# Recurrence, mLSTM and block attention as pieces between the chunks of one stream of projections

## The reference

```python
xn = rms_norm_2(x, mix_norm_g)
parts = split(xn @ w_in_2)           # LRU x, z | mLSTM u, o, z, two gates | block attention q, k, v, z
lru  = rg_lru_branch(...)            # causal conv, two block-diagonal gates, scan over the tokens, * silu(z)
ml   = mlstm_branch(...)             # conv, silu, block-diagonal q, k, v; 4 heads of 192, chunks of 128
                                     # tokens; * sigmoid(o), layer norm of each head, * silu(z)
moba = attention(q, k, v, alibi) * silu(z)    # 6 heads of 128, one block of 256 tokens
x = x + concat(lru, ml, moba) @ w_out_2
```

## Time and profile before

| | us |
|---|---|
| median of 3 runs (2581.98 to 2593.54) | 2593.01 |
| the profiled execution's own time | 2587.25 |
| its span in the profile | 2585.4 |
| PE busy in the span | 2109.4 (82%) |
| DVE, ACT, POOL busy | 1323.9, 631.1, 617.5 |
| mean granted clock of PE | 0.94 |
| DMA moved | 723 MB, 280 GB/s over the span |

### The profile page before, as it was taken

One profiled execution on the slowest core, in us unless ns is written; L12 is line 12 of the kernel. 1 busy time (PEld: TensorE's weight loads), 2 busy tenths in 40 slices (PEclk: granted clock), 3 DMA queues, 4 the chain that ended last, 5 costly groups with the idle time before them and its releaser, 6 DMA issues. The chain is left out here.

```text
span 2585.4 us, 22666 instructions
## 1 busy us (share of the span) xinstructions
PE 2109.4 (82%) x8289; PEld 1394.9 (54%) x8289; DVE 1323.9 (51%) x1822; ACT 631.1 (24%) x927; POOL 617.5 (24%) x518
## 2 busy tenths in 40 slices
PE   5999868974898899677778889977888999845976
PEld 4878656862444444222234444432348999834874
DVE  3456437457455546455665545654323344366544
ACT  4434235221101111111111110110023333343333
POOL 0000000016454354344454354444310000000000
PEclk8999969996999999899999999999989999967988
DMA  4555501479999999999999999999954455600432
GB/s 169 193 191 191 178 1 52 144 280 377 422 419 420 422 420 422 422 422 421 421 420 414 422 417 418 421 421 422 392 170 170 148 183 182 196 6 25 166 128 81
DMA packets 101560, 723.39 MB, mean 280 GB/s; under 512 B 11712, under 2 KB 12864, under 8 KB 20704
## 3 DMA queue, kind: packets, MB, share of 16 engines
q0 software_dynamic: 73728, 536.90, 50.4%
q1 hardware_dynamic: 27744, 185.32, 20.5%
HBM read 720.08 MB, written 2.10 MB: 279 GB/s over the span
## 5 line engine op out<-in xcount | busy, mean ns | idle before, releaser
L1164 PE MATMUL bank<-ring,work 128*128 128x512 f32 x2048 | 951.7, 610 | 237.0 <-DMA ring<-in_peer_up_dram,work 233.3
L1370 DVE CUSTOM_DVE_ANT_0 ring<-ring,mix_t 128x2048 f32<-128x2048 f32 x256 | 584.3, 2292 | 527.6 <-DMA ring<-in_peer_down_dram,work 527.5
L1164 PEld LDWEIGHTS bank<-ring,work 128*128 128x128 f32 x2048 | 376.3, 193 | 744.8 <-issue 542.7
L400 DVE TENSOR_TENSOR ring_r<-ring,ring_r 128x2048 fp32r<-128x2048 f32 (+2 forms) x160 | 321.7, 2013 | 386.1 <-ACT ring_r L378 385.9
L443 PE MATMUL bank<-ring_r,mix_r 128*128 128x512 f32 (+1 forms) x1440 | 449.4, 377 | 12.1 <-ACT h L341 12.1
L1267 POOL DMA_INDIRECT ring<-in_peer_down_dram,work x256 | 325.6, 1272 | 451.0 <-DVE work L1337 243.8
L1276 POOL DMA_INDIRECT ring<-in_peer_up_dram,work x256 | 289.8, 1132 | 523.3 <-PE bank L1164 459.7
L443 PE MATMUL bank<-ring_r,act_r 128*128 128x512 f32 (+1 forms) x1152 | 395.9, 384 | 18.9 <-DVE ring_r L400 18.9
L378 ACT ACTIVATE ring_r<-ring 128x2048 fp32r<-128x2048 f32 (+2 forms) x160 | 270.1, 1690 | 445.0 <-DMA ring<-in_w_out_dram 90.4
L443 PEld LDWEIGHTS bank<-ring_r,mix_r 128*128 128x128 f32 x1440 | 269.3, 189 | 54.8 <-ACT h L341 13.0
L1222 ACT ACTIVATE work<-const,work 128x128 f32<-128x128 f32 x256 | 97.7, 399 | 772.5 <-PE bank L1164 770.4
(11 more groups left out here) (326 smaller groups left out, 1112.0 us busy)
## 6 DMA issues: line engine op xcount, KB each, us to landing
ring<-in_w_out_dram SPq DMA_DIRECT2D x32, 1024.0 KB, 4.8
ring<-in_w_in_qk_dram SPq DMA_DIRECT2D x24, 1024.0 KB, 4.9
ring<-in_w_in_rest_dram SPq DMA_DIRECT2D x24, 1024.0 KB, 4.9
ring<-in_w_in_mo_dram SPq DMA_DIRECT2D x24, 768.0 KB, 4.3
ring<-in_w_in_tok_dram SPq DMA_DIRECT2D x24, 768.0 KB, 4.3
h<-in_w_query_dram SPq DMA_DIRECT2D x8, 2048.0 KB, 11.7
h<-in_xa_wkv_dram SPq DMA_DIRECT2D x4, 2048.0 KB, 16.8
ring<-in_w_in_lru_dram SPq DMA_DIRECT2D x8, 1024.0 KB, 4.8
```

The source lines that it names most:

```text
L400: dve.tensor_tensor(low(s, job), raw, plain(high(s, job)), ALU.subtract).then_inc(k.weights_low, 1)
L1164: m = pe.matmul(B[c][:, :], diag[:, j % DEPTH, :], up_row(j)[:, c * 512:(c + 1) * 512], start=first, stop=last)
L1370: dve.tensor_tensor_reduce(down_row(j), down_row(j), xn[:, t, :], 1.0, 0.0, ALU.mult, ALU.add, dots[:, p, j:j + 1]).then_inc(down_used, 1)
```

## The change

**One stream.** `Stream` lays out chunks in order, each with its slot, its banks and, for each bank, the count at which it is free; PE waits for a bank only where it opens it. All loops are unrolled; this form serves every projection of the program. "in2" and "out2" become one call of `project` with 80 chunks: gates 0 to 3, LRU 4 to 11, mLSTM u 12 to 19 (now three groups of 128 features, 36 matmuls), mLSTM o and z 20 to 31 (three tok blocks of 512), attention v 32 to 39, attention q, k, z for three heads and again for the other three 40 to 63, output 64 to 79 with two blocks by turns. It has banks 0 to 3; the last two output blocks take 4 to 7, which the pieces use until then. Banks are evacuated three chunks after a block's last one in program order (before: four).

**Pieces.** Each stage's engine programs become generators that yield the tick of their next piece. `runner` does what is due ahead of a chunk: PE at tick t ahead of chunk t, ACT and DVE at tick t ahead of the split of chunk t+3, SP ahead of the load of chunk t+3. The order on each engine is thus fixed.

**Ticks.** Recurrence: DVE 1, 3, 8 and 9 (convolution in halves), 15, 17, 18; PE 12; ACT 2, 13 (sigmoids), 14 (tanh, exp), 15 (silu), 16 (square root). mLSTM: PE 5, 10, 15, 17, 20, 22, 26 to 37, 47; DVE 2, 4, 6, 9, 11, 16, 19 to 24 (convolution in halves at 22 and 24), 28, 30 to 36, 38 to 40, 42, 44 to 46, 48; ACT 7, 20 to 22, 24, 26, 27, 29, 36, 37, 41, 43, 48. Recurrence's result is split at 49. Attention: scores at 51, 52, 53, 60, 61, 62, on DVE and ACT at the same ticks, division one later, transposes two, second product three later, gates at 55, 55, 56, 64 to 66, splits at 57 and 67.

**Memory.** The pieces work in `h`, `work` and in `x` itself, so SP stores the 2 MB of `x` to DRAM at tick 0 (with six small loads) and loads it back at tick 47, behind the 1.5 MB of alibi and a wait for the mLSTM result. The mixed activations are split where they lie, per piece. Where a query head's 192 rows end inside a chunk of 128, the product uses a half filled with zeros (`k_half`, cleared by POOL).

**Elsewhere.** The loads of the memory's query weights start with the normalisation ahead of it (before: at the end of "out2").

```diff
-def load_chunks(sp, k, job, b, n, groups_done):
...
+class Stream:
...
+    def __init__(self, k, order, banks=range(8), late_banks=None):
...
+        for job, b, s in order:
+            c = Chunk(job, b, s)
+            c.n, c.slot = k.chunks, k.chunks % CHUNKS
+            c.load_wait = k.slot_free[c.slot]
...
+    def runner(self, eng, programs):
+        tasks = [[0, program(eng)] for program in programs]
+
+        def at(tick):
+            for task in tasks:
+                while task[0] <= tick:
+                    task[0] = next(task[1], math.inf)
...
         def _(sp):
...
+            at, rest = beside.runner(sp, beside.load)
+            for p in range(len(chunks)):
+                at(p - AHEAD)
+                if p >= stream.started:
+                    stream.load(sp, p)
...
         def _(act):
...
+            for p in range(len(chunks) + AHEAD):
+                at(p - AHEAD)
...
+                for c in taken_at(p):
+                    if not c.job.add:
+                        take_out(act, c)
+                if p < len(chunks):
+                    c = chunks[p]
+
+                    act.wait_ge(k.loaded[c.slot], 16 * (c.n // CHUNKS + 1))
+                    act.activation(high(c), raw(c), ACT.Copy).then_inc(k.weights_high, 1)
...
         def _(pe):
...
+            at, rest = beside.runner(pe, beside.tensor)
+            for p, c in enumerate(chunks):
+                at(p)
...
+                for need in c.needs:
+                    pe.wait_ge(*need)
+
+                pe.wait_ge(k.weights_low, c.n + 1)
...
+                for q in range(4):
+                    for g, i in enumerate(c.banks):
+                        if c.opening and q == 0 and c.bank_waits[g] is not None:
+
+                            pe.wait_ge(*c.bank_waits[g])
...
-def rg_lru(k, ml, name="lru"):
...
+    def tensor(pe):
+        yield 12
+        pe.wait_ge(conv_done, 2)
+        pe.wait_ge(arrived, 48)
+        pe.wait_ge(sums_out, 1)
+        for c in range(CH):
+            for g, w in enumerate((wa, wx)):
+                m = pe.matmul(B[c][:, g * T:(g + 1) * T], w[:, c, :], xc[:, c, :], start=True, stop=True)
+            m.then_inc(gates_in, 1)
...
+        yield 10
+        pe.wait_ge(lf_done, 1)
...
+        yield 47
+        pe.wait_ge(y_done, NT)
...
+    def tensor_turn(pe):
+        for h, tick in enumerate(MOBA_TICKS):
+            yield tick + 2
+            pe.wait_ge(divided, 2 * h + 2)
...
+def residual_beside(k, beside, away, spilled, ml_done, back):
+
+    def load(sp):
+        yield 0
+        sp.dma_start(away, k.x[:, :]).then_inc(spilled, 16)
+        yield 47
+        sp.wait_ge(ml_done, NT)
+        sp.dma_start(k.x[:, :], away).then_inc(back, 16)
...
+    order = [c for job in (gates, lru, ml_u, ml_oz, mo_v, mo) for c in job.in_order()] + out2.in_pairs()
+    stream = Stream(k, order, banks=range(4), late_banks={(id(out2), 2): (4, 5), (id(out2), 3): (6, 7)})
...
+    for e in range(2):
+        for s, needs in enumerate(([(lru_low, 1)], [(ml_low, 2)], [(ml_low, 3), (mo_low, 1)], [(mo_low, 2)])):
+            stream.chunks[stream.at(out2, e, s)].needs = needs
+    out2.add_waits = [(back, 16)]
+    project(k, stream, "in2", split_act, beside=beside)
```

More of the change, by code:

```diff
@@ L254, in start_stream @@
[L254 to L290 removed]
+AHEAD = CHUNKS - 1
@@ L325, in project, with high @@
-    adds = jobs[0].add is not None
-    def with_activations(before, s):
-        return before is None and s < act_kc // 4
-    def take_out(eng, job, b, j, g):
-        for gi in range(job.groups):
-            eng.wait_ge(k.group_done, g + (gi + 1))
-            bank = k.banks[(b * job.groups + gi) % max(job.groups, 4) if job.unroll == 1 else j * job.groups + gi]
-            src = bank[:, 0:job.cols] if job.kind != "feat" else bank[0:job.keep, 0:T]
-            if adds:
-                m = eng.tensor_tensor(job.dest(b, gi), src, job.add(b, gi), ALU.add)
-            else:
-                m = eng.activation(job.dest(b, gi), src, ACT.Copy)
-            m.then_inc(k.group_out, 1)
+    def high(c):
+        return k.slots_r[:, CHUNKS + c.slot, 0:4 * c.job.cols]
@@ L402, in _ @@
-            last = over_blocks(dve, body)
-            if adds:
-                take_out(dve, *last)
-            if beside is not None:
-                beside.vector[jobs[-1].blocks](dve)
+            at, rest = beside.runner(dve, beside.vector)
+            for p in range(len(chunks) + AHEAD):
+                at(p - AHEAD)
+                if p < len(splits):
+                    src, hi, lo = splits[p]
+                    dve.wait_ge(act_high, p + 1)
+                    dve.tensor_tensor(lo, src, plain(hi), ALU.subtract).then_inc(act_low, 1)
+                for c in taken_at(p):
+                    if c.job.add:
+                        for need in c.job.add_waits:
+                            dve.wait_ge(*need)
+                        take_out(dve, c)
+                if p < len(chunks):
+                    c = chunks[p]
+                    dve.wait_ge(k.weights_high, c.n + 1)
+                    dve.tensor_tensor(low(c), raw(c), plain(high(c)), ALU.subtract).then_inc(k.weights_low, 1)
@@ L455, in normalise @@
+            rest(len(chunks))
 def normalise(k, name, src3, gain, dst3, load=None, upcoming=None, beside=None):
@@ new lines, in tensor, with turned_rows @@
+        yield 20
+        pe.wait_ge(*u_in[0])
+        pe.wait_ge(w_asked, 1)
+        values(0)
+        yield 22
+        pe.wait_ge(*u_in[1])
+        pe.wait_ge(topped, 2)
+        values(1)
+        def turned_rows(half, i, bank, done):
+            for b, cs in ((bank, HALVES[half][0:2]), (bank + 1, HALVES[half][2:3])):
+                for e, c in enumerate(cs):
+                    m = pe.matmul(B[b][:, e * T:(e + 1) * T], bd[:, i, c, :], uc[:, c, :], start=True, stop=True)
+                m.then_inc(done, 1)
```

1430 lines of the change are left out of this document (844 added, 586 removed).

## The result

The changed kernel takes 2486.96 us (median of 4 runs, 2482.3 to 2496.55), the kernel before, on the same chip, 2587.49 (4 runs, 2581.28 to 2593.54): ratio 0.9626, 95% interval 0.9603 to 0.9649, so 3.7% faster. Forecast: 2497, range 2462 to 2550, faster with 0.93. The profiled execution took 2488.84 us; its span is 2487.0 against 2585.4, 98.4 us less, where the sum had 96.5 less.

What follows compares the result with a forecast made beforehand. PE bounds the projections; between them no engine is full, a chain of short steps. 2587.25 - 163.5 (what goes) + 41 (PE's pieces) + 26 (waiting) = 2490.8, on the median's level 2497; range 2462 to 2550.

Steps and rivals of the forecast that it cites:

- The gap, 140.5 whole: Between the second block's last input-projection matmul and first output-projection matmul: 140.5 us go, as output chunks follow input chunks.
- Cold start 1.5: At the start of the second block's output projection: about 1.5 us go.
- boundaries 11.5: Where one projection job meets the next, in both blocks: per-bank waits remove PE's waits for evacuations, together 11.5 us.
- The regrouping, 10: mLSTM input in three groups of 128 instead of four of 96: 1.2 us less per chunk, 10 us.
- PE's pieces, 41: Matmuls and transposes of recurrence, mLSTM and attention on PE: 41 us, all on the path; bounds 36 and 64.
- Waiting, 26: PE's waits for late helpers and loads in the second block's stream, summed by place: 26 us, bounds 0 and 75.
- The 4 us for ticks 21 to 38: PE and DVE chained at each of these ticks, PE's own pieces giving the helper time: 4 us of waiting.
- The attention's wait: Probability needed two ticks after its score, with DVE work and an ACT evacuation behind an exp: 4 per three heads, 8.
- only long stalls are paid twice: PE's clock in the stream: a stall that lowers it costs about 1.7 us more; waits of 2.7 still show 1.00.
- More waits: Rival, chance 0.24: PE's waits delay loads and late helpers stay late, 1.3 us more at 38 pieces and lost clock: 2547.
- Fewer waits: Rival, chance 0.13: the 26 us of waiting vanish because helpers have slack: 2471 or a little less.
- No cover: Rival, chance 0.04: all 138 us of DVE and ACT pieces stand on the path, slower at 2609.

Runs made afterwards that it cites:

- without pieces: Changed kernel with recurrence, mLSTM, block attention and the residual's store left out beside the second block's 80 chunks, output reading the input activations: 2416.27 us, ratio 0.9336.
- added PE work: Changed kernel with each transpose of the second block's pieces, and each of their matmuls that opens an accumulation group, done twice: 2513.48 us, ratio 0.9723.
- kernel with job waits: Changed kernel in which PE waits at a job's first chunk for every group of the job before, as the kernel before did: 2494.31 us, ratio 0.9658.
- added DVE work: Changed kernel in which VectorE sums half of the chunk's weights ahead of each low split of the second block's 80 chunks: 2512.36 us, ratio 0.9708.

## Why the prediction was right

The direction, the mechanism and the size held: 2497 against 2487, in its range. Step by step, the forecast's number first:

- **What bounds the kernel.** Right: without pieces PE is busy 378 of 383 us, and 33.1 us of added PE work lengthen the stretch by 24.3; the rest comes back as shorter waits and less lost clock.
- **The gap, 140.5 whole.** Right. Put back, it measures 144.5.
- **Cold start 1.5, boundaries 11.5.** Putting the boundary waits back costs 11.0 us of the profiles; of these 1.8 are chunk 50's, so 9 to 11 for 11.5. With the pieces between them the projections take 4.7 us more than alone, where 1.5 was taken for the output's start; 2.3 of it is the output's first passes at the lower clock.
- **The regrouping, 10.** Alone it is worth 12.2 us (11 of work at the full clock), so mis-sized by a little; as a part of this change 3.3. The forecast had booked 10 of gain here and 4.5 of waits at ticks 12 to 20 as if they were independent. The difference, 5.5, is not far from 3.3; taken one by one the two terms meant little.
- **PE's pieces, 41.** 40.3: the price of a column and of a transpose came out of dense stretches elsewhere in the kernel, not from the half-clock windows, and that choice was right.
- **Waiting, 26.** By the rows 16.8, but everything that the pieces cost beyond PE's own time is 70.9-40.3 = 30.6 us. The list of places was nearly right (2.14 for 2.7 at tick 10, 1.33 for 1.4 at chunk 16, 2.37 for 3 at ticks 17 and 20, 2.24 for 1.5 at tick 47, 1.97 for 4.5 at chunk 50, 6.7 for 8 in the attention). The 4 us for ticks 21 to 38 were wrong: no wait there. Missing were 3.5 us at the start (0.5 taken), 5.0 at the borders of pieces, 2.3 of half clock and 1.3 of a slower 512-column pass: 11.6 that the forecast didn't have, against 8.4 by which the named waits fell short. The total was near partly by luck.
- **The attention's wait** was put down to 1.4 and 0.8 us of DVE and to one ACT evacuation behind an exp; in the changed kernel it is the ACT step that ends last. DVE's and ACT's rows at tick 53:

```profile
2231.66 0.68 DVE L2146 SCALAR_TENSOR_TENSOR work<-bank,h 128x512 f32<-128x512 f32 x1
2232.38 0.69 DVE L2149 TENSOR_REDUCE h<-work 128x2 f32<-128x512 f32 x1
```
```profile
2233.10 0.51 ACT L2182 ACTIVATE work<-work,h 128x256 f32<-128x256 f32 x1 [1.85 <-DVE h L2149]
...
2233.61 0.49 ACT L2182 ACTIVATE work<-work,h 128x256 f32<-128x256 f32 x1
...
2234.10 0.57 ACT L2191 ACTIVATE work<-bank 128x512 f32<-128x512 f32 x1
```

  Score and maximum on DVE, then two exponentials, and only then ACT copies the turned probabilities of another head that PE (2234.82) waits for: a copy standing behind a step that it has nothing to do with. Copied first, the wait goes to the next in line, the division: 3.77 became 2.81.
- **The clock.** The granted clock of the stretch is 0.98. The pair of matmuls behind the wait of 1.97 us lasts 0.50 us, the full level (2.4 GHz); behind 7.44, and behind the 3.78 us at chunk 50 of the kernel with job waits, 0.80, the lower one (1.2 GHz), which costs 1.6 and 2.3 us on the passes that follow. With the Trainium skill's statement ("TensorE: Matmul & The Clock Gate", Part 1) that activity releases the half rate, the trace agrees: PE works on behind each of these waits, and the granted clock goes back to 1.00. The forecast's reading that only long stalls are paid twice holds in part. Its own case, the wait of 2.6 us, was followed by a clock of 1.00, but waits of some 2.2 us go both ways. In the changed kernel the clock stays at 1.00 behind the 2.14 us at 1981.89 and drops behind the 2.24 us at 2191.66; in the kernel with job waits the same 2.14 us at tick 10 are followed by a drop. Windows behind these two, changed kernel first, with the row of the second wait:

```profile
2192.20:2195.50 3.30, 3.30 (x18) 3.30 (x16) 1.07 (x1) 0.00 (x0) 0.00 (x0) 0.50 0.86 287
```
```profile
1980.27 0.39 PE L1873 MATMUL bank<-work,const 128*128 128x8 f32 x2 [2.14 <-DVE work L1702]
1982.20:1985.50 3.30, 3.30 (x17) 3.30 (x17) 1.40 (x1) 1.48 (x1) 0.00 (x0) 0.50 0.00 0
```

  So the length of one wait doesn't tell by itself whether the clock falls, and what decides it stays open. The forecast's sum had no term for the clock; inside the stretch it takes 7.6 us, 5.4 more than without pieces.
- **The level.** The 5.8 us added for the median above the profiled run were wrong by as much: with one more run the median before is 2587.49, next to the profiled 2587.25. Without them the forecast is 2490.8, 3.8 from the measured one. Slips in the sum's working (seven steps of 41.87 us are 6.0 each, not 5.9; 88.3-86.6 is 1.7, not 1.5) are worth less than 1 us.
- **The rivals.** "More waits" (2547) is excluded: no wait stands at ticks 21 to 38, so the chained ticks there did not pass lateness on. "Fewer waits" (2471) is excluded too, as 30.6 us remain beyond PE's time. "No cover" is excluded by the added DVE work, of which two thirds vanish.

## What to carry to other kernels

When a chain of short steps runs beside a stream that fills one engine, its price is what it takes on that engine, plus waits, lost clock and borders that came to three quarters as much again: 40.3 and 30.6 us here, where the chain by itself held the path for 144.5. Shorten the stream's chunks and PE waits more for its helpers, lengthen them and the helpers catch up; a saving on the bound engine should be priced together with the waits of the helpers at the same place. To find the helper that is late, read the row ahead of the one that ends the wait: on an engine that works in order it is often held by another step, and moving one by a tick uncovers the next.

## What the runs showed of the hardware that was not expected

- 96 more matmuls in a stretch with 430 us of busy PE added 8.6 us of busy time but 3.3 us of length; the same 96 without pieces added 13.4 busy and 12.2 of length. At the full clock it is 11 us both times; busy time alone mixes work with the clock.
- Waits of 2.1 to 2.2 us of PE were followed by the lower clock in some places and not in others, the same wait (2.14 us at tick 10) included, while one of 2.58 us in the kernel before was not.
- The start-to-start distance of 512-column passes of the output projection and input was 227 ns by the median with no pieces, 229 with them. The activations lie in other buffers there, and DVE and ACT are busier; which of the two it is, if either, was not tried.
- A table load of ACT took 1.28 us with 0.01 to 0.02 us before the next activation, also in the middle of back-to-back work.
